# Segment sums of a Mamba-2 scan with a split moving operand, and y products that wait for their own head group

## The reference, cut to what matters

```python
adt = dt * a                                   # (tokens, 8 heads)
decay = exp(segsum(adt))                       # per head, 128 x 128 within a block of tokens, lower triangle
y_diag = einsum((C @ B^T) * decay, x * dt)     # inside the block
y_off  = einsum(C * exp(cumsum(adt)), state)   # from the blocks before
state  = exp(sum(adt)) * state + B^T @ (x * dt * to_end)
y = y_diag + y_off + D * x
```

## Time and profile before

| | us |
|---|---|
| three runs | 1161.8, 1159.23, 1161.77; median 1161.77 |
| profiled execution: its own time | 1160.59 |
| its span | 1158.8 |
| PE busy | 1100.1 (95% of the span) |
| DVE, ACT, POOL busy | 863.1, 536.2, 212.1 |
| mean granted TensorE clock | 0.974 of full speed |
| chain that ended last, by engine | PE 89%, DVE 4%, the others 2% or less |

### The profile page before, as it was taken

One profiled execution on the slowest core, in us unless ns is written; L12 is line 12 of the kernel. 1 busy time (PEld: TensorE's weight loads), 2 busy tenths in 40 slices (PEclk: granted clock), 3 DMA queues, 4 the chain that ended last, 5 costly groups with the idle time before them and its releaser, 6 DMA issues.

```text
span 1158.8 us, 14802 instructions
## 1 busy us (share of the span) xinstructions
PE 1100.1 (95%) x5176; PEld 895.5 (77%) x5176; DVE 863.1 (74%) x1089; ACT 536.2 (46%) x900; POOL 212.1 (18%) x203
## 2 busy tenths in 40 slices
PE   2699999999999999969999999999999999999997
PEld 2578877777787878757888888888888888888885
DVE  5779567657459566587988888888888886776687
ACT  3631144445444343466454444454445454454453
POOL 2100000000012333123333333333333100000012
PEclk7699999999999999988999999999999999999999
DMA  9989311001132111105344343434353496733224
GB/s 341 313 245 316 119 37 37 20 19 37 37 110 81 64 38 55 56 36 146 109 164 140 131 151 120 159 128 158 109 170 109 144 365 225 237 100 98 94 90 165
DMA packets 115293, 152.69 MB, mean 132 GB/s; under 512 B 15084, under 2 KB 75053, under 8 KB 115245
## 3 DMA queue, kind: packets, MB, share of 16 engines
q1 hardware_dynamic: 114925, 151.00, 38.8%
q0 software_dynamic: 320, 1.06, 0.3%
HBM read 121.10 MB, written 30.95 MB: 131 GB/s over the span
## 4 chain that ended last, share of the span: by engine, by line
PE 89%; DVE 4%; DMA 2%; ACT 2%; issue 1%; POOL 1%; SPq 1%; DVEq 0%; POOLq 0%; ACTq 0%
PE ps L2259 34%; PE ps L1912 25%; PE ps L2324 17%; PE ps L1978 2%; PE ps L1951 2%; PE ps L1965 1%; PE ps L2102 1%; PE ps L2017 1%; DVE big L1233 1%; DMA raw<-in_w_in_dram 1%; ACT big L956 1%; DMA scratch<-in_rel_bias_dram 1%; PE ps L2146 1%; PE ps L2194 1%; PE ps L2094 1%
## 5 line engine op out<-in xcount | busy, mean ns | idle before, releaser
L1912 PE MATMUL ps<-a_hi,w_hi 128*128 128x512 f32 x416 | 144.8, 426 | 8.0 <-DVE a_lo L1293 5.7
L1912 PE MATMUL ps<-a_lo,w_hi 128*128 128x512 f32 x416 | 132.4, 397 | 0.0
L1912 PE MATMUL ps<-a_hi,w_lo 128*128 128x512 f32 x416 | 131.3, 394 | 0.0
L2324 PE MATMUL ps<-w_hi,a_hi 128*128 128x512 f32 x308 | 119.9, 389 | 0.2 <-DVE a_lo L1745 0.2
L2324 PE MATMUL ps<-w_lo,a_hi 128*128 128x512 f32 x308 | 119.8, 389 | 0.0
L2324 PE MATMUL ps<-w_hi,a_lo 128*128 128x512 f32 x308 | 119.8, 389 | 0.0
L1145 ACT ACTIVATE w_hi<-raw 128x512 fp32r<-128x512 f32 x77 | 48.7, 632 | 98.4 <-PE ps L2324 88.3
L1912 PEld LDWEIGHTS ps<-a_hi,w_hi 128*128 128x128 f32 x416 | 73.2, 191 | 26.5 <-issue 16.3
L1912 PEld LDWEIGHTS ps<-a_hi,w_lo 128*128 128x128 f32 x416 | 79.2, 190 | 18.2
L1912 PEld LDWEIGHTS ps<-a_lo,w_hi 128*128 128x128 f32 x416 | 78.9, 190 | 17.9 <-issue 0.5
L1065 ACT ACTIVATE scratch<-ps 128x512 f32<-128x512 f32 x88 | 52.2, 593 | 84.8 <-PE ps L2259 84.8
(11 more groups left out here) (244 smaller groups left out, 2418.1 us busy)
## 6 DMA issues: line engine op xcount, KB each, us to landing
big<-in_w_ada_dram SPq DMA_DIRECT2D x24, 1024.0 KB, 8.8
raw<-in_w_up_dram SPq DMA_DIRECT2D x22, 512.0 KB, 5.1
big<-in_w_up_dram SPq DMA_DIRECT2D x22, 512.0 KB, 4.7
big<-in_w_down_dram SPq DMA_DIRECT2D x22, 512.0 KB, 6.4
down_weight_sums<-big SPq DMA_DIRECT2D x22, 512.0 KB, 3.4
raw<-down_weight_sums SPq DMA_DIRECT2D x44, 256.0 KB, 2.8
ffn_hidden<-big SPq DMA_DIRECT2D x21, 512.0 KB, 2.6
big<-ffn_hidden SPq DMA_DIRECT2D x21, 512.0 KB, 7.5
```

What stands on the lines that cost most here:

```text
L1912: mm = pe.matmul(out, lhs_of[a], rhs_of(b, j), start=first and p == 0, stop=last and p == 2)
L2324: mm = pe.matmul(bk, a[:, ts], rhs_op(s)[w], start=fresh and m == 0, stop=last and m == 2, skip_group_check=s // KH in (J6, J3, J7))
```

## The change

1. The moving operand of the segment sums is split. ACT copies `strict` and adt to float32r (`strict_r`, `adt_r[:, 0]`), POOL makes the rest `adt_r[:, 1]`, once, during the input projection. For each block and group POOL then writes two tiles, the hi and the lo terms, and PE multiplies both by `strict_r` into the same bank.
2. The terms lie in w_hi and w_lo, not in `decay`: block 0 in slot 1, all later blocks in slot 0. The mixed rows lie in slot 1 for blocks 0 to 6 and in slot 0 for block 7.
3. POOL waits before block i for `s_D` ≥ 2i (the segment sums of block i-1), before block 0 also for `s_wu` ≥ 18 (input unit 17 used up) and before block 1 for `s_wu` ≥ 19 (unit 18 used up).
4. `y_diag_products` waits for the weights of group 0, and ahead of the fifth head for those of group 1.
5. The four semaphores of the token sums become one that counts in program order.

```diff
+        small_r = sb("small_r", [P, 512], f32r)
+        strict_r = small_r[:, 0:P]
+        adt_r = small_r[:, P:2 * P].rearrange("p (v n) -> p v n", v=2)
...
+        def decay_term(i, part, g):
+            return (w_hi, w_lo)[part][:, 0 if i else 1, g * 512:(g + 1) * 512]
+        def mixed_op(b):
+            n = 1 if b < NB - 1 else 0
+            return w_hi[:, n, :], w_lo[:, n, :]
...
             def decay_terms(i):
                 if i >= 1:
-                    pool.wait_ge(s_yd, i)
+                    pool.wait_ge(s_D, 2 * i)
+                if i <= 1:
+                    pool.wait_ge(s_wu, U_OUT - 1 + i)
                 for g in range(GROUPS):
-                    adt = dtv[:, ADT, i * H + 4 * g:i * H + 4 * g + 4].unsqueeze(2).to_broadcast([P, 4, P])
-                    tri = upper.unsqueeze(1).to_broadcast([P, 4, P])
-                    pool.tensor_tensor(decay[:, g, :].rearrange("p (h l) -> p h l", h=4), tri, adt,
-                                       ALU.mult).then_inc(s_rd, 1)
-
-            pool.wait_ge(s_dte, 1)
+                    for part in range(2):
+                        adt = adt_r[:, part, i * H + 4 * g:i * H + 4 * g + 4].bitcast(f32).unsqueeze(2)\
+                            .to_broadcast([P, 4, P])
+                        tri = upper.unsqueeze(1).to_broadcast([P, 4, P])
+                        pool.tensor_tensor(decay_term(i, part, g).rearrange("p (h l) -> p h l", h=4), tri, adt,
+                                           ALU.mult).then_inc(s_rd, 1)
+            pool.wait_ge(s_ar, 2)
+            pool.tensor_tensor(adt_r[:, 1, :], dtv[:, ADT, :], adt_r[:, 0, :].bitcast(f32), ALU.subtract)\
+                .then_inc(s_ar, 1)
+            pool.wait_ge(s_ar, 3)
             decay_terms(0)
...
                 if n == U_DT + 2:
+                    act.wait_ge(s_dte, 1)
+                    act.activation(strict_r, strict, ACT.Copy).then_inc(s_ar, 1)
+                    act.activation(adt_r[:, 0, :], dtv[:, ADT, :], ACT.Copy).then_inc(s_ar, 1)
                     act.wait_ge(s_dt2, 1)
...
+            def segment_sums(i, g):
+                for part in range(2):
+                    pe.wait_ge(s_rd, 4 * i + 2 * g + part + 1)
+                    mm = pe.matmul(bank(5 + 2 * g), strict_r, decay_term(i, part, g), start=part == 0, stop=part == 1)
+                mm.then_inc(s_D, 1)
...
-                pe.wait_ge(s_rd, 2 * i + 1)
-                pe.matmul(bank(5), strict, decay[:, 0, :], start=True, stop=True).then_inc(s_D, 1)
+                segment_sums(i, 0)
             def second_sums(i):
                 pe.wait_ge(s_cbm, i + 1)
-                pe.wait_ge(s_rd, 2 * i + 2)
-                pe.matmul(bank(7), strict, decay[:, 1, :], start=True, stop=True).then_inc(s_D, 1)
+                segment_sums(i, 1)
...
             def y_diag_products(i):
                 pe.wait_ge(s_xc, i + 1)
-                pe.wait_ge(s_W, 2 * i + 2)
                 for h in range(H):
+                    if h % 4 == 0:
+                        pe.wait_ge(s_W, 2 * i + h // 4 + 1)
```

More of the change, by code:

```diff
@@ L127, in hybrid_layer_kernel @@
         s34_w = sb("s34_w", [P, 2, T], f32r)
-        sb("above_s34", [P, 2, T])
+        sb("above_s34", [P, 1536])
+        small_r = sb("small_r", [P, 512], f32r)
+        strict_r = small_r[:, 0:P]
+        adt_r = small_r[:, P:2 * P].rearrange("p (v n) -> p v n", v=2)
         gate_rows = sb("gate_rows", [P, 2, D])
@@ L242, in hybrid_layer_kernel, with sums_to @@
         N_SPLITS = len(TOKEN_SPLITS)
+        TOKEN_SUMS = [("t1", EARLY), ("t2", EARLY), ("t4", EARLY), ("t1", MIDDLE), ("t2", MIDDLE), ("t4", MIDDLE),
+                      ("t1", LATE), ("t2", LATE), ("t4", LATE), ("t3", EARLY), ("t3", REST)]
+        def sums_to(name, part):
+            return TOKEN_SUMS.index((name, part)) + 1
         def token_source(name):
@@ L367, in hybrid_layer_kernel @@
         s_dt1, s_dtA = sem("dt_steps_of_dve"), sem("dt_steps_of_act")
+        s_ar = sem("dt_a_split")
         s_dte, s_dtc, s_dt2 = sem("dt_a_ready"), sem("dt_a_sums_in_psum"), sem("dt_a_sums_taken")
@@ L389, in hybrid_layer_kernel @@
         s_hu = sem("h_tile_used_up")
-        s_t1, s_t2, s_t4 = sem("token_t1_summed"), sem("token_t2_summed"), sem("token_t4_summed")
-        s_t3 = sem("token_t3_summed")
+        s_tk = sem("token_sums_made")
         s_bh, s_bl = sem("token_operand_hi"), sem("token_operand_lo")
@@ L542, in _ @@
                     load_xr(b + 2)
-            sp.wait_ge(s_t3, 2)
+            sp.wait_ge(s_tk, sums_to("t3", REST))
             sp.wait_ge(s_bl, TOKEN_SPLITS.index(("t3", EARLY)))
@@ L981, in token_hi @@
                 if name in ("t1", "t2", "t4"):
-                    act.wait_ge({"t1": s_t1, "t2": s_t2, "t4": s_t4}[name], PARTS.index(part) + 1)
+                    act.wait_ge(s_tk, sums_to(name, part))
                     if part == EARLY:
@@ L988, in token_hi @@
                 elif name == "t3":
-                    act.wait_ge(s_t3, 1 if part == EARLY else 2)
+                    act.wait_ge(s_tk, sums_to(name, part))
                 act.activation(token_part(token_op(name)[0], part), token_part(token_source(name), part), ACT.Copy)\
@@ L1010, in _ @@
                     act.wait_ge(s_mT, i)
-                    act.activation(by_tile(ring(w_hi, U_OUT + i - 1)), by_tile(bank(2, 2)), ACT.Copy).then_inc(s_mh, 1)
+                    act.activation(by_tile(mixed_op(i - 1)[0]), by_tile(bank(2, 2)), ACT.Copy).then_inc(s_mh, 1)
                 if i == NB:
@@ L1532, in token_sum @@
                     dve.wait_ge(s_e2, 2 * blocks - 1)
-                    dve.tensor_tensor(t1_sum[:, :, c0:c1], b12, b11, ALU.subtract).then_inc(s_t1, 1)
+                    dve.tensor_tensor(t1_sum[:, :, c0:c1], b12, b11, ALU.subtract).then_inc(s_tk, 1)
                 elif name == "t2":
-                    dve.wait_ge(s_t1, n + 1)
+                    dve.wait_ge(s_tk, sums_to("t1", PARTS[n]))
                     dve.wait_ge(s_e2, 2 * blocks)
@@ L1538, in token_sum @@
                         dve.wait_ge(s_bl, 2)
-                    dve.tensor_tensor(b11, b22, t1_sum[:, :, c0:c1], ALU.subtract).then_inc(s_t2, 1)
+                    dve.tensor_tensor(b11, b22, t1_sum[:, :, c0:c1], ALU.subtract).then_inc(s_tk, 1)
                 else:
-                    dve.wait_ge(s_t2, n + 1)
+                    dve.wait_ge(s_tk, sums_to("t2", PARTS[n]))
                     if n == 0:
                         dve.wait_ge(s_bl, 4)
-                    dve.tensor_tensor(b21, b21, b11, ALU.subtract).then_inc(s_t4, 1)
+                    dve.tensor_tensor(b21, b21, b11, ALU.subtract).then_inc(s_tk, 1)
             def t3_sum(part):
@@ L1549, in t3_sum @@
                 b12 = x1nT[:, 0:4, 512 + c0:512 + c1]
-                dve.wait_ge(s_t1, PARTS.index(EARLY if part == EARLY else LATE) + 1)
-                dve.tensor_tensor(b12, x1nT[:, 4:8, 512 + c0:512 + c1], b12, ALU.subtract).then_inc(s_t3, 1)
+                dve.wait_ge(s_tk, sums_to("t1", EARLY if part == EARLY else LATE))
+                dve.tensor_tensor(b12, x1nT[:, 4:8, 512 + c0:512 + c1], b12, ALU.subtract).then_inc(s_tk, 1)
             def token_lo(n):
@@ L1602, in mixed_lo @@
                 dve.wait_ge(s_mh, b + 1)
-                u = U_OUT + b
-                dve.tensor_tensor(by_tile(ring(w_lo, u)), by_tile(bank(2, 2)), by_tile(ring(w_hi, u).bitcast(f32)),
+                dve.tensor_tensor(by_tile(mixed_op(b)[1]), by_tile(bank(2, 2)), by_tile(mixed_op(b)[0].bitcast(f32)),
                                   ALU.subtract).then_inc(s_ml, 1)
@@ L2176, in project_out @@
                     mm = split_products([bank(out_bank(b) + hf) for hf in range(2)],
-                                        (ring(w_hi, u)[:, cs], ring(w_lo, u)[:, cs]),
+                                        [op[:, cs] for op in mixed_op(b)],
                                         lambda s, j: (a_hi, a_lo)[s][:, k, j * 512:(j + 1) * 512],
```

## The result

Over 20 runs of each kernel the median went from 1162.42 to 1164.36 us; the ratio is 1.0016, with a 95% interval of 1.0008 to 1.0023. The change made the kernel 1.9 us slower, where the sum had 0.9 us faster and the forecast for the median was 1160.3 (1156.0 to 1163.8). The difference is small, but clear of the scatter with 20 runs of each. The profiled execution took 1162.87 us with a span of 1161.1, 2.3 more than before.

A forecast was written before the change was run, and what follows sets the result against it. PE was taken to bound a turn, except 4.76 us set by ACT and DVE. First sums -2.4 and turn 1 +1.5 gave -0.9 us: 1159.7 for the profiled execution, median 1160.3 (1156.0 to 1163.8).

The forecast's parts named there:

- First sums: First segment sums in turns 2 to 7, where PE bounds: 0.40 us saved in each of six turns, -2.4 us.
- Second sums: Second segment sums in turns 2 to 7: 0.40 us shorter inside 4.76 us set by ACT and DVE, gain 0.
- y products: y products waiting by group: avoids a 0.2 us PE stall, but PE then waits for `mixed_lo` anyway, gain 0.
- POOL in turns 2 to 7: Four POOL terms instead of two, at 1.26 us each, lateness absorbed by idle time behind them: cost 0.
- Block 0: POOL's later terms hidden by 4 us; both sums lie between PE-bound matmuls, so the last unit ends 0.8 us earlier.
- Turn 1: POOL's block 1 terms wait for unit 18, delaying `ssm_rows(0)` and DVE's work: `project_out(0)` at 356.3 instead of 354.77, +1.5 us.
- three DVE operations pay 0.23 each, 0.7 in all: Turn 1: two weight products and `w_out_lo(2)` slowed beside POOL's block 2 terms, 0.7 us in all.
- its fall as something that would break it: Sign against the sum: granted clock falling between 346 and 357, where PE idles more than before; no size given.
- rival B: DVE waits for whole POOL terms: 3.1 for 0.7 in turn 1, L1521 late in five turns; +2.0, 1162.6 us, chance 0.12.
- turn 1's lower bound: Turn 1 with POOL terms of 1.02 us each and no pull on DVE: `project_out(0)` +0.5 us.
- its upper: Turn 1 with POOL terms of 2.04 us each: `project_out(0)` +5.2 us.
- A: PE keeps all it saves: both sums count in the turns, turn 1 costs nothing; -6.4, 1154.2 us, chance 0.16.

The follow-up runs named there:

- the halves of `mixed_lo`: DVE makes the lo part of the mixed rows in two halves: 0.9937 of before on top of both edits, 0.9964 on the kernel before.
- the run with block 2's terms later, at full clock: Changed kernel with block 2's terms after block 1's y products and useless PE products filling turn 1's gaps: 0.9993 of before.
- the filled one: Changed kernel with useless float32 products on PE in all three gaps of turn 1: 1.0008 of before.
- both edits: Changed kernel with block 1's terms in slot 1, made right after block 0's sums, and block 2's terms after block 1's y products: 0.997 of before.
- The first two experiments: Changed kernel with block 1's terms in slot 1, made right after block 0's sums: 1.0012; changed kernel with block 2's terms after block 1's y products: 1.0006.
- the second experiment: Changed kernel in which POOL starts block 2's terms only after the y products of block 1: 1.0006 of before.

## Why the prediction was wrong, point by point

*First sums*, -2.4 us: right. Turns 2 to 7 brought 2.36 us (4.56 late at `project_out(0)`, 2.20 at the last). The agreement is a little better than the reasoning: five turns brought 0.36 each, since the split matmuls behind the longer wait took 3.00 instead of 2.97 us, and the way from `project_out(0)` to turn 2 brought 0.57, of which 0.15 are split matmuls that had no wait ahead of them (2.82 instead of 2.97).

*Second sums*, 0: right. The chain through ACT and DVE set the turn, and the halves of `mixed_lo` showed that nothing else stood there. PE's wait grew from 0.31 to 0.86 us and not to the 0.7 forecast, because the y products became 0.15 shorter.

*y products*, 0: right for the time, in both directions: alone nothing, with `mixed_lo` in halves 0.06 us a turn. That they themselves went from 1.88 to 1.73 us was not foreseen, and the wait hid it.

*POOL in turns 2 to 7*, 0: right (from turn 4 into 5 the four terms ran from 421.40 to 425.92, and the root behind them still waited for ACT). *Block 0*, -0.8: right (the chains of both executions come to the first sums at 334.5, and the state product follows 0.82 us sooner).

*Turn 1*, +1.5 us at `project_out(0)`: this step failed; it measured +4.56. Its first half held: POOL at 345.33 (345.2 forecast), the terms done at 349.8 (349.8), `ssm_rows(0)` at 350.88 (350.8). Without the next term the sum gave 355.6, 12.2 us after the state product; the run with block 2's terms later, at full clock, took 12.2. The term that was mis-sized is "three DVE operations pay 0.23 each, 0.7 in all". At full clock it was 3.1 us: `ssm_rows(0)`, which the sum had not counted at all as standing beside POOL, paid 2.43 - 0.88 = 1.55, and the two weight products 2.97 - 1.29 = 1.68; `w_out_lo(2)` paid nothing. (These make 3.2; in the run to compare with, the filling held `mixed_lo` up by 0.15.) The rest is the clock, for which the sum had no term, though the prediction named its fall as something that would break it: `project_out(0)` came 15.92 us after the state product in the changed kernel and 15.30 in the filled one, 0.6 us.

Two misreadings lie behind it, and both can be shown. The first: the forecast took the earlier trace rows to say that DVE's L1587 ran undisturbed "in the middle of POOL's two terms". That row merges two records. Asked for shorter windows, the trace of the kernel before gives them one by one:

```profile
418.10 1.04 POOL L698 TENSOR_TENSOR scratch<-sq,dtv 128x512 f32<-128x512 f32 x1
419.10 1.52 POOL L698 TENSOR_TENSOR scratch<-sq,dtv 128x512 f32<-128x512 f32 x1
```

The first term ended at 419.1 and L1587 began at 419.04: it stood between the two terms, and the second took 1.52 us instead of 1.04. The changed kernel has the same in the same place:

```profile
381.74 1.05 POOL L718 TENSOR_TENSOR w_hi<-sq,small_r 128x512 fp32r<-128x512 f32 x1
382.74 1.56 POOL L718 TENSOR_TENSOR w_lo<-sq,small_r 128x512 fp32r<-128x512 f32 x1
...
382.71 0.69 DVE L1613 TENSOR_TENSOR big<-big 128x512 f32<-128x512 f32 x1
```

The second: the price of 0.23 us an operation came from L1441 at 409.26. The instruction of POOL beside it was nearly over:

```profile
408.34 1.29 POOL L725 TENSOR_TENSOR big<-raw 128x512 f32<-128x512 f32 x1
```

It ended at 409.63, 0.37 us after L1441 began, so the row shows the rest of one wait and not what an operation pays that meets a whole term.

So rival B had the mechanism: it priced the turn 1 collision at 3.1 us (3.1 measured) and was given 0.12. That the two figures agree is in part luck, since B counted two weight products and `w_out_lo(2)`, and it was two `ssm_rows` records and two weight products that paid. Its other half, L1521 waiting for the fourth term, did not happen: L1521 took 0.92 instead of 0.75 us and held nobody. The Trainium skill, "SBUF — State Buffer", section "SBUF: two separate sides", describes a lock by which the one that starts second waits for the other's whole instruction. The rows of turn 1 agree (1.26 us for a first `ssm_rows` record of 0.48, started 0.05 behind a term of 1.03). I had set that aside for one row read wrongly.

The chances for slower came out small because the forecast counted only losses of more than 0.3% as slower, and B's +2.0 was within it. Small slips of the sum change nothing: turn 1's lower bound adds up to +0.4 and not +0.5, its upper to +5.1 and not +5.2, and 1156.0 lies more than half way from the forecast to A.

What stays open: how often the clock falls in turn 1. Behind the same gap of 1.4 us it fell in one profiled execution (both edits) and not in another (with the halves), and the timed runs carry no clock by stage. The first two experiments did on DVE what was expected and missed in time. In the profiled execution of each the clock had fallen; that it fell in their timed runs too is likely and not shown.

**What beats both.** Both edits and the halves: 0.9937 of before (0.9923 to 0.995), a median of 1154.5 us beside 1162.67.

## What to carry to other kernels

When work is made for an engine that is far from the bound, look at what stands behind it in its queue and at whom it runs beside: POOL at 20% busy cost 4.4 us here at full clock, about half by order and half by the company it kept, while PE had 4 us less to do. Where a stage has slack in every turn but one (a first turn written out, with operands that come free late), give that turn a row of its own in the sum. And before a row is taken as evidence that two instructions do not disturb each other, ask for their single records: a merged row hides where one ended. A price taken from a row where the two meet only for the end of one is too low.

## What the runs showed of the hardware that was not expected

- The first group of twelve split matmuls of `project_out` took 2.80 to 2.87 us when it followed the y products without a wait, and 2.96 to 3.01 after a wait of 0.3 to 0.9 us. A short wait of PE cost 0.15 us more than its length here.
- The y products of turns 2 to 7 took 1.88 us behind one wait for both groups' weights and 1.73 with a wait for each group, in a kernel that differed in nothing else (1.97 where the one wait had held PE for 0.14 us).
- The granted clock went to its lower level after PE gaps of 1.4 us in one execution (both edits) and stayed full after the same gap in another (with the halves). Where it fell, it stayed down for about 3 to 10 us (349.5 to 352.9 with both edits, 349.8 to 360 in the second experiment).
- POOL's terms written as float32r took the 1.0 us of those in plain float32.
